# Attention outputs formed turned in half lanes, weighed by small spreading products

## The chip, the cores and the metric

The kernel runs on one core of a Trainium2 chip, as one program. TensorE (PE in the profile) multiplies, VectorE (DVE) and ScalarE (ACT) work element by element and empty PSUM, SyncE (SP) issues transfers. The metric is device time in microseconds of that core: the median of 3 runs.

## The reference

The program computes two blocks on 256 tokens of width 1024. The first is a block with a state space mixer, an attention with forget gates and a mixture of experts. The second has two layers, and each layer has three attention mixers, whose outputs go through projections and gates, and then a cross attention and a feed-forward part. The change is inside the three mixers of the second block, so it runs once in each of the two layers. What they compute for one block of 128 queries, cut to its core:

```python
def masked_probs(s, mask, sink=None):
    ...
    e = jnp.exp(s - m)
    denom = jnp.sum(e, axis=-1, keepdims=True)
    if sink is not None:
        denom = denom + jnp.exp(sink - m)
    return e / jnp.where(denom > 0, denom, 1.0)

# swa (8 heads of 64, 2 key heads), window 128
o = einsum('bgrqk,bkgd->bqgrd', masked_probs(s, mask, sink), vb)
# nsa: three branches, each weighed by a gate of its own
return g[..., 0:1] * o_cmp + g[..., 1:2] * o_sel + g[..., 2:3] * o_win
# mla: 8 heads
return einsum('bhqk,bkhd->bqhd', masked_probs(s, kpos <= t), v)
```

So each head's output is a product of unnormalised weights with the values, times one factor for each query and head: the reciprocal of the sum, and for the nsa branches the gate as well.

## The kernel before, in words

Each engine has a queue written out by hand (for TensorE from L659, ScalarE from L1829, VectorE from L2276); counting semaphores tie them. A PSUM bank is a `Bank` with two counters: `full`, raised by the engine that filled it, and `free`, raised by the one that emptied it; `claim(b, ...)` waits until the bank's last user is done. The bank of the outputs is O, that of the scores S (two banks), that of the turned weights PT (two banks), and X is a spare one.

The mixers of a layer are a pipeline of 18 steps, `MIXER_STEPS`: swa 0 to 3, sel 4 to 7, cmp 8 and 9, win 10 to 13, mla 14 to 17. A step is a kind, a group of four heads (`pp`) and a block of 128 queries (`qb`). Steps with `qb` 0 have one block of 128 keys, those with `qb` 1 two. The two cmp steps do all 8 heads on 16 compressed keys each.

TensorE does at step n, in this order: `mixer_turn(n)` transposes the weights of step n (L775, cmp L1314), the scores of step n+2 (L763), one or more `gate_part`s of 12 products of 128x512 each (L1282; these are a part of the gate projection and fill the time in which the others work), and `mixer_output(n)`: the outputs of step n (`output_step`, L785). There the turned weights of 128 keys x 128 queries are the stationary operand and 64 value columns move, so the output has queries in the lanes and head columns along a row. The cmp steps have one product of 128x512 (L1322). An fp32 product shows as two matmul records in the trace, a transpose as one.

VectorE does at step n: for a cmp step `total_blocks` (L3153 to L3160: sum, reciprocal, gate), `mixer_mask(n+2)` (L2366, L2369: scores with mask, and row maxima), `mixer_finish(n)` (`finish_step`: reciprocal L2390, gate L2394, and the multiply L2404 that empties O; cmp L3167, L3169), then the low parts of the gate weights (`make_gate_low`, L3074, one for each gate part of step n+2). Extra pieces stand at single steps: at step 0 the eight L3108, at step 15 `make_low("bra")`, a pass of 128x4096 over the weights of the first branch projection (L2314). ScalarE does the exponentials of step n+1 (L1900), empties PT (L2191) and the gate banks (L2170), and makes the high parts of the weights (L2145, L1876).

Behind the last step TensorE transposes the three finished outputs (L691, `turn_rows`), 8 blocks each in pairs of banks X and O, ScalarE rounds each to its high part (`turned_high`, L1887), VectorE takes the low part (`turned_low`, L2305), and TensorE starts the branch projections (L718, `product_wide`), "bra" first.

## Time and profile before

| | us |
|---|---|
| median of 3 runs | 1678.88 (1677.71 to 1680.25) |
| profiled execution | 1675.22 |
| its span | 1673.5 |
| TensorE busy | 1590.7 (95%) |
| VectorE busy | 939.6 (56%) |
| ScalarE busy | 654.3 (39%) |

The mean granted clock of TensorE is 0.988 of full speed. The first block ends near 577 us, the two layers of the second follow, near 577 to 1117 and 1117 to 1673. The mixer pipeline of the first layer lies at about 690 to 818 us, that of the second at 1228 to 1357. A row of the timeline has a start, a length, an engine, a line of the kernel, the operation and its tiles, and a count; a bracket at its end is idle time of the engine before it and what ended it. Successive matmuls overlap in the records, so their pitch (the distance of two starts) tells the rate, not their length.

### The profile page before, as it was taken

To read this page: it belongs to the slowest core of one execution; us is meant where nothing else is said; L and a number is where in the kernel's file an instruction comes from. 1 tells how busy PE (TensorE), PEld (TensorE's weight loads), DVE (VectorE), ACT (ScalarE), POOL (GpSimd) and SP (SyncE) were. 2 spreads that over 40 slices of the span, in tenths; PEclk is the share of its full clock that TensorE was granted. 3 is DMA by queue.
4 is the path that set the end of the run, shared out by engine and by line. 5 is a ranking of instruction groups with operands and counts; after the bars stand their busy time and mean duration, and the time that the engine had idled before them with its cause. 6 is when DMAs were issued, how large, how long until landed. Compare 5 with 4: busy or idle time off the path is not lost.

```text
span 1673.5 us, 22371 instructions
## 1 busy us (share of the span) xinstructions
PE 1590.7 (95%) x9359; PEld 1237.3 (74%) x9359; DVE 939.6 (56%) x1374; ACT 654.3 (39%) x960; POOL 27.1 (2%) x89
## 2 busy tenths in 40 slices
PE   5999999989999899999999999999999999999998
PEld 1998655454545377687888899978768878889986
DVE  3876676642222465556675566545466567556653
ACT  2543411111111243556545544335265744543441
POOL 1000010100000000000000000000000000000000
PEclk9999999999999999999999999999999999999999
DMA  9555519979999943333345355545424235435551
GB/s 309 189 186 201 202 52 332 386 289 414 411 423 381 353 142 129 102 137 109 133 152 180 123 192 172 191 154 192 154 76 152 101 130 191 157 130 185 202 181 71
DMA packets 153155, 333.33 MB, mean 199 GB/s; under 512 B 17764, under 2 KB 69222, under 8 KB 140774
## 3 DMA queue, kind: packets, MB, share of 16 engines
q1 hardware_dynamic: 147504, 326.94, 53.9%
q10 hardware_dynamic: 5558, 5.06, 0.9%
q8 instruction: 70, 1.15, 0.3%
q14 instruction: 23, 0.18, 0.0%
HBM read 330.94 MB, written 1.05 MB: 198 GB/s over the span
## 4 chain that ended last, share of the span: by engine, by line
PE 81%; DVE 9%; DMA 4%; ACT 4%; issue 1%; POOL 0%; ACTq 0%; POOLq 0%; DVEq 0%; SPq 0%
PE ps_g L737 19%; PE ps_g L718 15%; PE ps_g L1142 6%; PE ps_g L1282 6%; PE ps_s L1538 4%; PE ps_p L1538 3%; PE ps_o L785 3%; PE ps_g L878 3%; DVE ring_r L2314 2%; PE ps_p L718 2%; PE ps_o L1171 2%; DMA ring<-in_w_mod_dram 1%; PE ps_x L1171 1%; PE ps_p L775 1%; DMA arena<-in_w_up_dram 1%
## 5 line engine op out<-in xcount | busy, mean ns | idle before, releaser
L2314 DVE TENSOR_TENSOR ring_r<-ring,late_w 128x4096 fp32r<-128x4096 f32 (+1 forms) x50 | 216.9, 4339 | 153.3 <-ACT late_w L1876 153.3
L1876 ACT ACTIVATE late_w<-ring 128x4096 fp32r<-128x4096 f32 (+1 forms) x50 | 178.2, 3563 | 126.7 <-PE ps_p L1538 42.8
L737 PE MATMUL ps_g<-hf_high,ring_r 128*128 128x256 f32 x640 | 179.0, 280 | 0.0
L737 PE MATMUL ps_g<-hf_high,late_w 128*128 128x256 f32 x576 | 162.1, 281 | 0.0
L737 PE MATMUL ps_g<-h_t_r,late_w 128*128 128x256 f32 x576 | 161.3, 280 | 0.0
L737 PEld LDWEIGHTS ps_g<-hf_high,ring_r 128*128 128x128 f32 x640 | 122.0, 191 | 0.0
L737 PEld LDWEIGHTS ps_g<-h_t_r,late_w 128*128 128x128 f32 x576 | 108.6, 189 | 0.0
L737 PEld LDWEIGHTS ps_g<-hf_high,late_w 128*128 128x128 f32 x576 | 108.1, 188 | 0.0
L1900 ACT ACTIVATE arena<-arena,neg_max 128x256 f32<-128x256 f32 (+1 forms) x160 | 71.5, 450 | 40.9 <-DVE neg_max L2369 40.9
L1142 PE MATMUL ps_g<-arena 128*64 128x512 f32 x288 | 83.9, 592 | 0.0
L718 PE MATMUL ps_g<-early_w,first_low 128*128 128x512 f32 (+1 forms) x176 | 68.7, 390 | 3.8 <-ACT arena L1862 1.8
L785 PEld LDWEIGHTS ps_o<-arena 128*128 128x128 f32 x496 | 61.4, 192 | 13.2 <-issue 9.1
L1282 PE MATMUL ps_g<-gate_w,first_low 128*128 128x512 f32 x160 | 67.4, 421 | 1.6 <-ACT arena L2170 1.6
L718 PE MATMUL ps_g<-early_w,h_t_r 128*128 128x512 f32 (+1 forms) x176 | 68.6, 390 | 0.0
L2314 DVE TENSOR_TENSOR ring_r<-ring,early_w 128x4096 fp32r<-128x4096 f32 (+2 forms) x12 | 47.6, 3968 | 36.9 <-ACT early_w L1876 36.9
L718 PE MATMUL ps_g<-ring_r,first_low 128*128 128x512 f32 (+1 forms) x176 | 68.2, 387 | 0.0
L785 PE MATMUL ps_o<-arena 128*128 128x64 f32 (+1 forms) x496 | 61.5, 273 | 6.3 <-ACT arena L1915 3.1
L1282 PE MATMUL ps_g<-gate_w,h_t_r 128*128 128x512 f32 x160 | 63.1, 394 | 0.0
L1282 PE MATMUL ps_g<-ring_r,first_low 128*128 128x512 f32 x160 | 62.9, 393 | 0.0
L2314 DVE TENSOR_TENSOR ring_r<-ring,first_w 128x4096 fp32r<-128x4096 f32 x11 | 48.7, 4426 | 25.0 <-ACT first_w L1876 25.0
L3074 DVE TENSOR_TENSOR ring_r<-ring,gate_w 128x1024 fp32r<-128x1024 f32 x40 | 48.4, 1219 | 24.3 <-ACT gate_w L2145 23.9
L1142 PE MATMUL ps_g<-ring,arena 128*64 128x512 f32 x192 | 55.6, 593 | 2.3 <-issue 2.3
(697 smaller groups left out, 3707.1 us busy)
## 6 DMA issues: line engine op xcount, KB each, us to landing
...
```

Source lines behind the costliest of these rows:

```text
L718: ins = pe.matmul(b.ap[:, 0:n], x[:, k, tb * P:(tb + 1) * P], a[:, k, lo:lo + n], start=k == 0 and i == 0, stop=k == nk - 1 and i == len(b ...
L737: ins = pe.matmul(b.ap[:, (f % 2) * SEQ:(f % 2 + 1) * SEQ], a[:, k, f * P:(f + 1) * P], x[:, k, :], start=k == 0 and i == 0, stop=k == nk ...
L785: ins = pe.matmul(O.ap[:, i * width:(i + 1) * width], probs_t[:, i, b, :], v(step, i, b), start=b == 0, stop=b == kbs - 1)
L878: ins = pe.matmul(b.ap[:, :], x[:, k, tb * P:(tb + 1) * P], w[:, k, :], start=k == 0, stop=k == KD - 1)
L1142: ins = pe.matmul(b.ap[lanes, :], taken_t[:, k, lanes], w[k], start=k == 0, stop=k == KD - 1)
L1171: ins = pe.matmul(y.ap[lanes, :], hid_t[:, k, lanes], wd[:, k, half * HALF:(half + 1) * HALF], start=k == 0, stop=k == KF - 1)
L1282: ins = pe.matmul(G[tb].ap[:, :], x[:, 2 * q + k, tb * P:(tb + 1) * P], a[:, k, :], start=q == 0 and k == 0 and i == 0, stop=q == KD // 2 ...
L1538: ins = pe.matmul((S, PT)[tb].ap[:, half * HALF:(half + 1) * HALF], a[:, k, tb * P:(tb + 1) * P], x[:, k - 4 * c, half * HALF:(half + 1) * ...
L1876: act.activation(high_of(name, rnd)[:, 0:n], ring[:, slot, 0:n], ACT.Copy).then_inc(high_ready.sem, 1)
L1900: ins = act.activation(s, s, ACT.Exp, bias=neg_max[:, n % 2, i:i + 1], scale=-1.0, accum_out=den[:, n % 4, i:i + 1])
L2314: dve.tensor_tensor(ring_r[:, slot, 0:n], ring[:, slot, 0:n], high_of(name, rnd)[:, 0:n].bitcast(F32), ALU.subtract).then_inc(low_ready.se ...
L3074: dve.tensor_tensor(gate_piece(name, q, ring_r), gate_piece(name, q, ring), gate_high_w[q].bitcast(F32), ALU.subtract).then_inc(gate_low, 1)
```

## The change

The outputs are formed turned. In `turned_output` the 64 value columns of a head are the stationary operand and the turned weights of 128 queries move; the result has head columns in the lanes and queries along a row. Even heads of a group go to lanes 0 to 63 and odd ones to lanes 64 to 127, so two heads share the columns of one product. As a query's factor now differs along the row and not by lane, it has to be spread over lanes: four more products per step have the factor of a head, one number for each query, broadcast over 64 columns as stationary operand, and the identity moves. They write columns 256 to 511 of O. VectorE forms the factors ahead (`mixer_inverse`), and TensorE waits for them (`inverse_ready`) ahead of these four. `mixer_finish` then copies the spread factors to SBUF and multiplies (L3237, L3240 of the changed kernel; win adds a third operation) where it multiplied once.

The cmp steps scale the weights before they are turned (L3184), so the transposition of step 8 and 9 waits for `blocks_scaled`, and their output is four products of 128x128. The finished outputs lie turned in `heads_t`; the 24 transpositions of a layer behind the mixers go, ScalarE and VectorE take high and low part from SBUF, and the first branch projection waits for `heads_low_ready`. The banks' counts of uses change with that (`LAYER_USES`: O 45 to 42, X 30 to 27).

```diff
...
@@ -1309,9 +1312,27 @@
                     if step[0] != "cmp":
                         turn_probs("layer", step, l)
                         return
-                    pe.wait_ge(probs.sem, probs.at("layer", step_tag(step), l))
+                    pe.wait_ge(blocks_scaled, len(CMP_STEPS) * l + CMP_STEPS.index(step) + 1)
                     claim(PT, step_tag(step), l)
                     pe.transpose(PT.ap[:, 0:P], scores[:, n % 2, 0, 0:P], ident[:, :]).then_inc(PT.full, 1)
+
+                def turned_output(step, v):
+
+                    tag, kbs = step_tag(step), keys_of(step) // P
+                    claim(O, tag, l)
+                    pe.wait_ge(PT.free, PT.nth("layer", tag, l))
+                    for c in range(2):
+                        for b in range(kbs):
+                            for half in range(2):
+                                pe.matmul(O.ap[half * HD:(half + 1) * HD, c * P:(c + 1) * P], v(2 * c + half, b), probs_t[:, 2 * c + half, b, :],
+                                          start=b == 0, stop=b == kbs - 1)
+                    pe.wait_ge(inverse_ready, len(WEIGHED) * l + WEIGHED.index(step) + 1)
+                    inverse = rden[:, MIXER_STEPS.index(step) % 2, 0:4]
+                    for i in range(4):
+                        half, c = i % 2, 2 + i // 2
+                        ins = pe.matmul(O.ap[half * HD:(half + 1) * HD, c * P:(c + 1) * P], inverse[:, i:i + 1].broadcast_to([P, HD]), ident[:, :],
+                                        start=True, stop=True)
+                    ins.then_inc(O.full, 1)
 
...
@@ -1319,13 +1340,15 @@
                     if step[0] == "cmp":
                         claim(O, step_tag(step), l)
                         pe.wait_ge(PT.free, PT.nth("layer", step_tag(step), l))
-                        pe.matmul(O.ap[:, :], probs_t[:, 0, 0, :], cmp_v[:, :, :].rearrange("p h d -> p (h d)"), start=True, stop=True)\
-                            .then_inc(O.full, 1)
+                        v = cmp_v[:, :, :].rearrange("p h d -> p (h d)")
+                        for c in range(KF):
+                            ins = pe.matmul(O.ap[:, c * P:(c + 1) * P], v[:, c * P:(c + 1) * P], probs_t[:, 0, 0, :], start=True, stop=True)
+                        ins.then_inc(O.full, 1)
                     elif step[0] == "mla":
-                        output_step("layer", step, lambda s, i, b: mla_v[:, b, (4 * s[1] + i) * HD:(4 * s[1] + i + 1) * HD], l)
+                        turned_output(step, lambda i, b: mla_v[:, b, (4 * step[1] + i) * HD:(4 * step[1] + i + 1) * HD])
                     else:
                         at_v = {"swa": C_AV, "sel": C_VS, "win": C_VW}[step[0]]
-                        output_step("layer", step, lambda s, i, b: proj[:, b, at_v + HD * (i // 2):at_v + HD * (i // 2 + 1)], l)
+                        turned_output(step, lambda i, b: proj[:, b, at_v + HD * (i // 2):at_v + HD * (i // 2 + 1)])
...
@@ -1373,12 +1396,6 @@
                     mixer_output(n)
 
 
-                for name, src in (("a", o_a), ("b", o_b), ("c", o_c)):
-                    if name == "b":
-                        pe.wait_ge(rows.sem, rows.at("layer", "ob", l))
-                    else:
-                        pe.wait_ge(O.free, O.nth("layer", step_tag((SWA_STEPS if name == "a" else MLA_STEPS)[-1]), l))
-                    turn_rows(f"o{name}", [lambda tb, k=k, s=src: s[:, tb, k * P:(k + 1) * P] for k in range(KF)], l)
...
-                for name in "ab":
-                    turned("layer", f"o{name}", 2, l)
+                for i, name in enumerate("ab"):
+                    pe.wait_ge(heads_low_ready, 6 * l + 2 * i + 2)
                     product_wide("layer", f"br{name}", (o_high[name], o_low[name]), l)
...
-                turned("layer", "oc", 2, l)
+                pe.wait_ge(heads_low_ready, 6 * l + 6)
...
@@ -2209,7 +2226,12 @@
                 act.wait_ge(O.full, O.nth("layer", step_tag(MLA_STEPS[-1]), l))
                 act.dma_start(mem_rows[:, :, :], t["mem_2"][0].rearrange("(b p) n -> p b n", p=P)).then_inc(in_mem, 16)
                 for name in "abc":
-                    turned_high(f"o{name}", KF, o_high[name], l)
+                    if name == "b":
+                        act.wait_ge(rows.sem, rows.at("layer", "ob", l))
+                    else:
+                        act.wait_ge(O.free, O.nth("layer", step_tag((SWA_STEPS if name == "a" else MLA_STEPS)[-1]), l))
+                    for r in range(2):
+                        act.activation(o_high[name][:, 2 * r:2 * r + 2, :], heads_t[name][:, 2 * r:2 * r + 2, :], ACT.Copy).then_inc(x_high.sem, 1)
...
@@ -3159,15 +3181,37 @@
...
+                    dve.tensor_tensor(block_scores(n), block_scores(n), over(rden[:, n % 2, :], CMP), ALU.mult).then_inc(blocks_scaled, 1)
+
+                def block_of(step, chunks):
+                    return heads_t["b" if step[0] in ("sel", "cmp", "win") else "a" if step[0] == "swa" else "c"][:, chunks, step[2] * P:(step[2] + 1) * P]
 
                 def finish_blocks(n, step):
 
-                    tag, o = step_tag(step), o_b[:, step[2], :].rearrange("p (h d) -> p h d", d=HD)
+                    tag, o = step_tag(step), block_of(step, slice(0, KF))
+                    dve.wait_ge(O.free, O.nth("layer", step_tag(MIXER_STEPS[n - 1]), l))
                     dve.wait_ge(O.full, O.nth("layer", tag, l))
-                    dve.tensor_tensor(cmp_tmp, O.ap[:, :].rearrange("p (h d) -> p h d", d=HD), over(rden[:, n % 2, :], HD), ALU.mult).then_inc(O.free, 1)
+                    dve.tensor_tensor(o, o, O.ap[:, :].rearrange("p (c q) -> p c q", q=P), ALU.add).then_inc(O.free, 1)
                     dve.wait_ge(O.free, O.nth("layer", tag, l))
-                    st.done(dve.tensor_tensor(o, o, cmp_tmp, ALU.add))
-                    st.settle()
+
+                def mixer_inverse(n):
+
+                    step = MIXER_STEPS[n]
+                    if step[0] == "cmp":
+                        total_blocks(n, step)
+                        return
+                    total, inv = den[:, n % 4, 0:4], rden[:, n % 2, 0:4]
+                    dve.wait_ge(probs.sem, probs.at("layer", step_tag(step), l))
+                    if step[0] == "swa":
+                        st.done(dve.tensor_tensor(total, total, sink_e[:, n % 4, 4:8], ALU.add))
+                        st.settle()
+                    ins = dve.reciprocal(inv, total)
+                    if step[0] in ("sel", "win"):
+                        st.done(ins)
+                        st.settle()
+                        inv4 = inv.rearrange("p (f r) -> p f r", f=2)
+                        ins = dve.tensor_tensor(inv4, inv4, branch(1 + (step[0] == "win"), step), ALU.mult)
+                    ins.then_inc(inverse_ready, 1)
...
                 def mixer_finish(n):
 
                     step = MIXER_STEPS[n]
-                    if step[0] == "swa":
-                        finish_step("layer", step, crossed(o_a)(step), l)
-                    elif step[0] == "sel":
-                        finish_step("layer", step, crossed(o_b)(step), l, branch(1, step), first=True)
-                    elif step[0] == "cmp":
+                    if step[0] == "cmp":
                         finish_blocks(n, step)
-                    elif step[0] == "win":
-                        ins = finish_step("layer", step, crossed(o_b)(step), l, branch(2, step))
-                        if step == WIN_STEPS[-1]:
-                            ins.then_inc(rows.sem, 1)
-                        else:
-                            st.done(ins)
-                            st.settle()
+                        return
+                    pp = step[1]
+                    out_t = block_of(step, slice(2 * pp, 2 * pp + 2) if step[0] == "mla" else slice(pp, KF, 2))
+                    dve.wait_ge(O.full, O.nth("layer", step_tag(step), l))
+                    sums, weight = (O.ap[:, i * SEQ:(i + 1) * SEQ].rearrange("p (c q) -> p c q", q=P) for i in range(2))
+                    st.done(dve.tensor_copy(o_tmp[:, :, :], weight))
+                    st.settle()
+                    if step[0] != "win":
+                        dve.tensor_tensor(out_t, sums, o_tmp[:, :, :], ALU.mult).then_inc(O.free, 1)
+                        return
+                    dve.tensor_tensor(o_tmp[:, :, :], sums, o_tmp[:, :, :], ALU.mult).then_inc(O.free, 1)
+                    dve.wait_ge(O.free, O.nth("layer", step_tag(step), l))
+                    ins = dve.tensor_tensor(out_t, out_t, o_tmp[:, :, :], ALU.add)
+                    if step == WIN_STEPS[-1]:
+                        ins.then_inc(rows.sem, 1)
                     else:
-                        finish_step("layer", step, o_c[:, step[2], step[1] * SEQ:(step[1] + 1) * SEQ].rearrange("p (i d) -> p i d", d=HD), l)
+                        st.done(ins)
+                        st.settle()
...
                 for n, step in enumerate(MIXER_STEPS):
-                    if step[0] == "cmp":
-                        total_blocks(n, step)
+                    mixer_inverse(n)
                     if n + 2 < len(MIXER_STEPS):
                         mixer_mask(n + 2)
                     mixer_finish(n)
...
                 for name in "abc":
-                    turned_low(f"o{name}", KF, o_low[name], o_high[name], l)
+                    for r in range(2):
+                        dve.wait_ge(x_high.sem, x_high.at("layer", f"o{name}{r}", l))
+                        dve.tensor_tensor(o_low[name][:, 2 * r:2 * r + 2, :], heads_t[name][:, 2 * r:2 * r + 2, :],
+                                          o_high[name][:, 2 * r:2 * r + 2, :].bitcast(F32), ALU.subtract).then_inc(heads_low_ready, 1)
...
```

Lines of the changed kernel are shifted: L785 answers to L1327 and L1333, L1314 to L1317, L1322 to L1345, L763 to L766, L1282 to L1285, L3074 to L3096, L2404 to L3237 and L3240, L2314 to L2336.

TensorE at the end of step 7 and the start of step 8, before:

```order
L785 MATMUL ps_o<-arena 128x64 [waits p_free,o_free]
L785 MATMUL ps_o<-arena 128x64 x7
L1314 MATMUL ps_p<-ident,arena 128x128 [waits p_free,probs_ready]
L763 MATMUL ps_s<-arena 128x128 [waits s_free]
L763 MATMUL ps_s<-arena 128x128 x3
```

and after:

```order
L1327 MATMUL ps_o<-arena 64x128 [waits p_free,o_free]
L1327 MATMUL ps_o<-arena 64x128 x7
L1333 MATMUL ps_o<-ident,rden 64x128 [waits inverse_ready]
L1333 MATMUL ps_o<-ident,rden 64x128 x3
L1317 MATMUL ps_p<-ident,arena 128x128 [waits p_free,blocks_scaled]
L766 MATMUL ps_s<-arena 128x128 [waits s_free]
L766 MATMUL ps_s<-arena 128x128 x3
```

Eight products of step 7 have become twelve, and the transposition of step 8 now waits for VectorE's scaling instead of the exponentials.

VectorE at the same place, from `mixer_finish(7)` on, before:

```order
L2404 TENSOR_TENSOR arena<-ps_o,rden 128x2x128 [waits o_full,vector_steps]
L3074 TENSOR_TENSOR ring_r<-ring,gate_w_64 128x1024 [waits gate_high]
L3153 TENSOR_REDUCE den<-arena 128x8 [waits probs_ready]
L3155 TENSOR_SCALAR den<-den 128x8 [waits vector_steps]
L3157 RECIPROCAL rden<-den 128x8 [waits vector_steps]
L3160 TENSOR_TENSOR rden<-rden,branch_g 128x8 [waits vector_steps]
L2366 SCALAR_TENSOR_TENSOR arena<-ps_s,causal 128x4x128 [waits s_full,vector_steps]
L2369 TENSOR_REDUCE neg_max<-arena 128x4 [waits s_free]
L3167 TENSOR_TENSOR arena<-ps_o,rden 128x512 [waits o_full]
```

and after:

```order
L3237 COPY arena<-ps_o 128x256 [waits o_full]
L3240 TENSOR_TENSOR arena<-ps_o,arena 128x2x128 [waits vector_steps]
L3096 TENSOR_TENSOR ring_r<-ring,gate_w_64 128x1024 [waits gate_high]
L3175 TENSOR_REDUCE den<-arena 128x8 [waits probs_ready]
L3177 TENSOR_SCALAR den<-den 128x8 [waits vector_steps]
L3179 RECIPROCAL rden<-den 128x8 [waits vector_steps]
L3182 TENSOR_TENSOR rden<-rden,branch_g 128x8 [waits vector_steps]
L3184 TENSOR_TENSOR arena<-arena,rden 128x128 [waits vector_steps]
L2388 SCALAR_TENSOR_TENSOR arena<-ps_s,causal 128x4x128 [waits s_full]
L2391 TENSOR_REDUCE neg_max<-arena 128x4 [waits s_free]
L3194 TENSOR_TENSOR arena<-arena,ps_o 128x4x128 [waits o_full,o_free]
```

The scaling L3184 stands behind the finish of step 7 and a gate weight pass; before, the transposition of step 8 waited for nothing in this queue.

VectorE at steps 15 to 17 (`late_w_56` holds the weights of "bra"), after:

```order
L3237 COPY arena<-ps_o 128x256 [waits o_full]
L3240 TENSOR_TENSOR arena<-ps_o,arena 128x2x128 [waits vector_steps]
L3096 TENSOR_TENSOR ring_r<-ring,gate_w_66 128x1024 [waits gate_high]
L2336 TENSOR_TENSOR ring_r<-ring,late_w_56 128x4096 [waits high_ready]
L3208 RECIPROCAL rden<-den 128x4 [waits probs_ready]
L3237 COPY arena<-ps_o 128x256 [waits o_full]
L3240 TENSOR_TENSOR arena<-ps_o,arena 128x2x128 [waits vector_steps]
```

The reciprocal L3208 is that of step 16, behind the pass over the weights, as it was before; new is that TensorE's products of step 16 wait for it.

## Rows read from the trace of the kernel before

**Rows 1.** Windows, mixers: us, busy PE, PEld, DVE, ACT, POOL, clock, DMA, GB/s.

```profile
690.00:818.00 128.00, 121.57 (x814) 101.45 (x815) 81.99 (x143) 78.10 (x198) 0.00 (x0) 1.00 0.28 102
1228.00:1357.00 129.00, 122.97 (x814) 102.55 (x811) 82.13 (x144) 78.04 (x198) 0.00 (x0) 0.99 0.28 102
```

**Rows 2.** Chain, end of the first layer's mixers: start, us, what.

```profile
800.80 1.73 PE ps_o L785 x16
...
802.98 2.77 PE ps_g L1282 x12
805.75 0.84 PE ps_o L785 x8
```

**Rows 3.** Timeline, TensorE: full-width and half-width products; start, us, engine, line, tiles, xcount.

```profile
303.04 18.19 PE L878 MATMUL ps_g<-ring,arena 128*128 128x512 f32 x42
...
382.72 7.04 PE L1142 MATMUL ps_g<-arena 128*64 128x512 f32 x32
```

**Rows 4.** Timeline, TensorE, from half-wide to full-wide tiles.

```profile
709.76 0.51 PE L1282 MATMUL ps_g<-gate_w,first_low 128*128 128x512 f32 x1
710.10 0.39 PE L1282 MATMUL ps_g<-ring_r,first_low 128*128 128x512 f32 x1
```

**Rows 5.** Timeline, steps 7 and 8 of the mixers.

```profile
741.16 0.29 DVE L3148 TENSOR_TENSOR arena<-arena,neg_max 128x128 f32<-128x128 f32 x1
...
743.88 0.28 PE L1314 MATMUL ps_p<-ident,arena 128*128 128x128 f32 x1
...
744.15 0.42 DVE L2404 TENSOR_TENSOR arena<-ps_o,rden 128x256 f32<-128x256 f32 x1 [2.41 <-PE ps_o L785]
...
744.49 1.21 DVE L3074 TENSOR_TENSOR ring_r<-ring,gate_w 128x1024 fp32r<-128x1024 f32 x1
...
745.62 0.28 DVE L3153 TENSOR_REDUCE den<-arena 128x8 f32<-128x128 f32 x1
...
746.58 0.69 DVE L2366 SCALAR_TENSOR_TENSOR arena<-ps_s,causal 128x512 f32<-128x512 f32 x1
```

**Rows 6.** Timeline, steps 8 to 10.

```profile
751.25 0.27 PE L1314 MATMUL ps_p<-ident,arena 128*128 128x128 f32 x1
...
751.45 0.69 DVE L3167 TENSOR_TENSOR arena<-ps_o,rden 128x512 f32<-128x512 f32 x1 [3.46 <-PE ps_o L1322]
...
757.42 0.71 PE L763 MATMUL ps_s<-arena 64*128 64x128 f32 x8 [0.56 <-DVE arena L2366]
...
761.94 0.47 PE L1282 MATMUL ps_g<-gate_w,first_low 128*128 128x512 f32 x1 [0.81 <-ACT arena L2170]
```

**Rows 7.** Timeline, steps 15 to 17 and the first branch products.

```profile
804.12 4.42 DVE L2314 TENSOR_TENSOR ring_r<-ring,late_w 128x4096 fp32r<-128x4096 f32 x1
...
811.83 0.61 PE L691 MATMUL ps_x<-ident,arena 128*128 128x128 f32 x4
...
812.50 0.60 ACT L1887 ACTIVATE oa_high<-ps_x 128x512 fp32r<-128x512 f32 x1 [1.51 <-PE ps_x L691]
...
817.14 0.48 PE L718 MATMUL ps_g<-late_w,oa_high 128*128 128x512 f32 x1
...
821.57 4.43 DVE L2314 TENSOR_TENSOR ring_r<-ring,late_w 128x4096 fp32r<-128x4096 f32 x1 [2.83 <-ACT late_w L1876]
...
828.41 0.40 PE L718 MATMUL ps_g<-late_w,ob_high 128*128 128x512 f32 x1
```

**Rows 8.** Timeline, steps 0 and 1.

```profile
699.38 4.49 DVE L3108 TENSOR_TENSOR arena<-arena,g_col 64x256 f32<-64x256 f32 x8
...
705.26 0.71 PE L763 MATMUL ps_s<-arena 64*128 64x128 f32 x8 [0.39 <-DVE arena L2366]
```

**Rows 9.** Windows, second layer, TensorE at half clock.

```profile
1235.20:1238.60 3.40, 3.40 (x17) 2.90 (x18) 2.83 (x5) 2.88 (x12) 0.00 (x0) 0.50 0.00 0
```

**Rows 10.** Timeline, TensorE, first output of the first and the second layer.

```profile
696.72 1.08 PE L785 MATMUL ps_o<-arena 128*128 128x64 f32 x8 [1.52 <-ACT arena L2191]
...
1234.42 1.21 PE L785 MATMUL ps_o<-arena 128*128 128x64 f32 x8 [1.51 <-ACT arena L2191]
```

9 lines of the change are left out of this document (6 added, 3 removed).

## The prediction

> **What bounds the kernel now.** I first read the windows over the two mixer pipelines: TensorE is busy 121.6 of 128 us and 123.0 of 129, VectorE 82 and ScalarE 78 [rows 1]. So the pipelines move at TensorE's pace, and what TensorE gains or loses there shows, unless a wait for another engine takes it back. The two layers read alike, so I work out the first and double it. Second I read the chain of waits at the pipeline's end: it runs from one TensorE group to the next, 1.73 us for the output products of a step with two key blocks, 0.84 for one [rows 2]. Third, the timeline at the places where the order of instructions changes: steps 0 and 1, 7 to 9, and 15 to the first branch product. TensorE has little idle time there, and what it has is small (0.39, 0.56, 0.81 us) [rows 6, 8]. Everything below is on TensorE's own timeline; a plus is time lost.
>
> **The change part by part, one layer.**
>
> *A, the products.* Of the 16 weighed steps, 8 have two key blocks and 8 one. Before, 16 records in 1.73 us and 8 in 0.84, thus 0.107 each [rows 2]. After, two halves of the lanes are written in turn. Whether they run side by side is told by the nearest products of this kind: 32 of 128x512 into half the columns took 7.04 us, 0.22 each, where 42 of full width took 18.19, 0.43 each [rows 3]; a pair of halves costs what one full product does. So a pair with 128 columns moving takes 0.11. A step with two blocks has 8 products for the sums and 4 for the factors, two records each: 12 pairs, 1.32 us; with one block 8 pairs, 0.88. To this comes the change of tile width, twice per step. After half-wide products, the first full-wide one was followed at 0.34 us [rows 4], where the steady pitch is 2.77/12 = 0.23 [rows 2]: 0.11 for that alone, and as much again is possible ahead of the first. I take 0.31 per step for both changes, bounds 0 and 0.5. That gives 1.63 against 1.73 and 1.19 against 0.84: 8 x (-0.10) + 8 x 0.35 = +2.0. The cmp outputs become 8 records of about 0.11 for about as much time, +0.1 for both. A is +2.1; with no cost for the change of width -2.9, with 0.5 it is +5.1, and with halves that run one after the other (0.107 each, so 2.6 and 1.7 us and the same 0.31) +16.5.
>
> The Trainium skill (TensorEngine Tiling (Array Packing), Performance Considerations) advises exactly such a swap of the stationary and the moving operand where the moving side has 64 columns, for twice the rate. By it alone, with no factors and no change of width to pay, the products would take half of 1.73 and 0.84, some 10 us less per layer. The same page (Key Properties) says that changing the tiling mode drains the engine: a cost that each of these short groups pays twice. The trace agrees with both as far as it goes, by the 0.22 and the 0.34 above.
>
> *B, the wait of the cmp steps.* The transposition of step 8 now waits for the scaling on VectorE. Ahead of it VectorE has the finish of step 7, which can only begin when TensorE has ended step 7's products, one instruction before the transposition. Read from rows: VectorE saw the end of the products 0.27 us after TensorE went on (744.15 against 743.88); the multiply took 0.34 to the next start, the gate pass 1.13, the four small ones 0.96 [rows 5]. After the change: 0.27, a copy of the same size with the wait of the multiply for it (0.45), 0.34, 1.13, 0.96, and the scaling, for which the subtraction of the same 128x128 took 0.29 [rows 5]: 3.45 us in which TensorE stands. Queued behind the transposition are the scores of step 10 and the gate products, which could run. Step 9 likewise: 0.20 to VectorE's start (751.45 against 751.25), the finish 0.73, two gate passes 2.27, 0.96, 0.30: 4.45 [rows 5, 6]. Two waits of TensorE just behind, 0.56 for VectorE and 0.81 for ScalarE, whose reason is that those engines lag, go with it [rows 6]: -1.4. B is +6.5. From below it is bounded by 0, were VectorE ahead; from above by 7.9, without the part given back.
>
> *C, the factors of step 16.* Its reciprocal stands behind the weight pass of 4.42 us, begun at 804.12 [rows 7], now some 0.4 later. Before, nobody but VectorE cared. Now the four spreading products wait. TensorE's output of step 16 begins at 805.75 [rows 2] and gets through the sums at 806.3; the pass ends at 808.95 and the reciprocal near 809.2. C is +2.9, bounds 2 and 3.5.
>
> *D, steps 0 and 1.* Eight small operations hold VectorE from 699.38 for 4.49 us, and TensorE waits 0.39 for the mask behind them [rows 8]. The copy ahead of them (0.45) and the reciprocal with the addition of the sink, which now stand ahead of that mask (0.4), come on top: +0.85. At step 12 the transpositions for mla claim the bank O, which a finish longer by the copy's 0.45 frees: +0.3. In the other steps the finish and the factors have the 2.8 to 5.5 us of gate products as cover; VectorE has 46 idle us, and the longer finish costs it some 16 x 0.45 = 7.
>
> *E, the end.* The 24 transpositions, in TensorE's way with waits for the banks, lasted from 811.83 to 817.14: 5.3 us. In their place TensorE waits behind its last product for the first high part, which ScalarE began 0.67 later (812.50) and did in 0.60, and then two low parts of 0.69 on VectorE, as long as its pass over 128x512 [rows 6, 7]: near 2.7 with the handovers. VectorE's copy and multiply of step 17 (0.27 + 0.8) lie beside ScalarE's part. E is -2.6. Late next would be the weights of the second branch: their low pass began 4.4 us after the first branch product (821.57 against 817.14), took 4.43, and was wanted at 828.41, 2.4 us later than it ended [rows 7]. ScalarE now has all six high parts after that point, which takes about 0.8 of the 2.4. So the gain stays.
>
> Sum: 2.1 + 6.5 + 2.9 + 1.15 - 2.6 = +10.05 us per layer.
>
> *F, the clock.* The three new stalls are 3.5, 4.5 and 2.9 us, longer than any in the pipeline now. In the second layer TensorE idled 1.51 us before its first output; from 1235.2 the granted clock was 0.50, that is 1.2 GHz, for 3.4 us. In the first layer 1.52 us idle at the same place had no such effect [rows 1, 9, 10]. One fall costs half of 3.4, 1.7 us. With idle times two to three times as long I count a fall after two of the three stalls: +3.4 per layer, bounds 0 and 5.1. (The Trainium skill, TensorE: Matmul & The Clock Gate, likewise has the clock fall to half after idling, and so speaks against an edit that trades work for waits.)
>
> Two layers: 2 x (10.05 + 3.4) = +26.9 us. The profiled execution, 1675.2, would become 1702.1. The median of the timed runs lies 3.7 above the profiled one; on that basis 1678.9 + 26.9 = 1705.8, and I say 1706.
>
> **The rivals.**
>
> *The clock holds.* For it: the first layer's 1.52 us. Then 2 x 10.05, 1699.0.
>
> *The halves don't run side by side* for such short products. The rows for it are of 512 columns; at 128 the weight load, not the moving side, sets the pitch, and the trace has no half-wide product of 128 columns. Then A is 16.5 in place of 2.1: 2 x (24.45 + 3.4) = +55.7, 1734.6.
>
> *VectorE is ahead and none of its new waits bites: not slower.* The place is the queue of VectorE between O's filling and the scaling of step 8 and 9, and the pass ahead of step 16. If its work is finished whenever TensorE asks, B, C and D fall away: 2.1 - 2.6 = -0.5 per layer, 1677.9, no change; if the change of width were free besides, 2 x -5.5, 1667.9. It decides from the point where the scaling ends 3.4 us earlier than I have it. For it speaks only VectorE's 46 idle us; against it the queue's order, in which the scaling stands behind a finish that needs the product just ended.
>
> *The stalls are given back*, partly. TensorE waits at step 8, but VectorE and ScalarE catch up, and later waits in the pipeline shrink. I counted 1.4; if 3 us more per layer come back and the clock falls once, 2 x (7.05 + 1.7) = +17.5, 1696.4.
>
> **How the numbers follow.** The forecast 0.48, the clock holds 0.2, stalls given back 0.16, halves in series 0.09, VectorE ahead 0.07. The range must hold the first three with their bounds: low 1691 (given back and no fall: 1678.9 + 2 x 7.05 = 1693, less 2 for A), high 1721 (A at +5.1 and three falls: 2 x (13.05 + 5.1) = +36.3 gives 1715, and 6 for what the queue's delay costs elsewhere). A measurement tells this kernel from no change at about 0.2%, 3.4 us. Faster by more: 0.03, the part of the last rival with free changes of width. Within: 0.04, its other part. Slower: 0.93.
>
> **What would show it.** At step 8 and 9 TensorE idle for 3.5 and 4.5 us before L1317, ended by VectorE; at step 16 idle for near 3 us between the sums L1327 and the spreading products L1333; the records of a two-block step in 1.6 us; the first branch product 2.7 us after the last output; granted clock 0.50 in some stretches behind the stalls. I would be wrong if a group of 16 half-wide records took 1.7 us by itself (halves in series), or if the idle time before L1317 were under 1 us.

## The result

The changed kernel takes 1708.89 us (median of 6 runs, 1706.79 to 1711.23), the kernel before 1678.61 us in the same series: 1.018 of it, interval 1.0165 to 1.0194. That is 30.3 us slower. The forecast was 1706, and 26.9 us slower.

The page of the changed kernel, part 1: TensorE has 15.7 us more of busy time, the span is 36.0 us longer.

```profile
PE 1606.4 (94%) x9591; PEld 1234.9 (72%) x9591; DVE 950.3 (56%) x1406; ACT 653.8 (38%) x960; POOL 27.1 (2%) x89
```

The profiled execution of before lay at the short end of its runs (1675.2), and this one took 1711.2. To tell the layers from that, I match VectorE's passes over the split weights (L2314 before, L2336 after), of which both kernels have the same number in the same order. The timeline of VectorE, first before, then after: the last such pass ahead of the first layer's mixers, one behind them, the last one ahead of the second layer's, and one behind those.

```profile
636.39 4.13 DVE L2314 TENSOR_TENSOR ring_r<-ring,early_w 128x3808 fp32r<-128x3808 f32 x1 [7.08 <-ACT early_w L1876]
...
857.15 4.42 DVE L2314 TENSOR_TENSOR ring_r<-ring,late_w 128x4096 fp32r<-128x4096 f32 x1
...
1172.19 4.13 DVE L2314 TENSOR_TENSOR ring_r<-ring,early_w 128x3808 fp32r<-128x3808 f32 x1 [5.65 <-ACT early_w L1876]
...
1384.83 4.42 DVE L2314 TENSOR_TENSOR ring_r<-ring,late_w 128x4096 fp32r<-128x4096 f32 x1
```

```profile
639.78 4.13 DVE L2336 TENSOR_TENSOR ring_r<-ring,early_w 128x3808 fp32r<-128x3808 f32 x1 [7.08 <-ACT early_w L1893]
...
875.96 4.42 DVE L2336 TENSOR_TENSOR ring_r<-ring,late_w 128x4096 fp32r<-128x4096 f32 x1
...
1190.81 4.13 DVE L2336 TENSOR_TENSOR ring_r<-ring,early_w 128x3808 fp32r<-128x3808 f32 x1 [5.63 <-ACT early_w L1893]
...
1420.90 4.41 DVE L2336 TENSOR_TENSOR ring_r<-ring,late_w 128x4096 fp32r<-128x4096 f32 x1
```

The distances are 3.4, 18.8, 18.6 and 36.1 us. So 3.4 us arose in code that the change doesn't touch, 15.2 us from the first of these passes to the third, the first layer's stretch, and 17.4 from the third to the fourth, the second's. These two numbers, taken between far passes, are what I use below for a layer. Together they are 32.7 us, more than the 30.3 of the medians: the profiled execution of before is 3.4 us under its median, that of the changed kernel 2.3 us above.

The windows of the changed kernel: the first layer's mixers as a whole, and then four short stretches in them (us, busy of PE, PEld, DVE, ACT, POOL, granted clock, DMA share, GB/s).

```profile
690.00:835.00 145.00, 127.94 (x949) 100.50 (x949) 88.46 (x165) 79.71 (x200) 0.00 (x0) 0.95 0.24 83
748.30:751.80 3.50, 0.30 (x6) 0.05 (x2) 2.98 (x8) 0.70 (x2) 0.00 (x0) 1.00 0.94 329
752.80:756.20 3.40, 3.40 (x11) 2.66 (x10) 1.38 (x2) 0.67 (x1) 0.00 (x0) 0.54 1.06 393
765.40:769.80 4.40, 4.33 (x14) 2.90 (x15) 1.78 (x3) 1.22 (x2) 0.00 (x0) 0.50 0.00 0
825.20:828.20 3.00, 3.00 (x13) 2.76 (x12) 0.93 (x3) 0.99 (x1) 0.00 (x0) 0.51 0.01 3
```

TensorE was busy 121.6 of 128 us before [rows 1]; now it is idle for 17 of 145. The second row is one of the new waits: TensorE stands, VectorE works through 2.98 of 3.5 us. The last three rows lie directly behind such waits, and there the granted clock is 0.50 to 0.54 of full speed, 1.2 GHz.

The timeline at the end of step 7 and in steps 8 and 9, to be read beside [rows 5] and [rows 6]:

```profile
748.64 0.42 DVE L3237 COPY arena<-ps_o 128x256 f32<-128x256 f32 x1 [1.85 <-PE ps_o L1333]
...
751.53 0.29 DVE L3184 TENSOR_TENSOR arena<-arena,rden 128x128 f32<-128x128 f32 x1
...
751.88 0.33 PE L1317 MATMUL ps_p<-ident,arena 128*128 128x128 f32 x1 [3.29 <-DVE arena L3184]
...
761.17 0.69 DVE L3194 TENSOR_TENSOR arena<-arena,ps_o 128x512 f32<-128x512 f32 x1 [6.86 <-PE ps_o L1345]
...
765.13 0.29 DVE L3184 TENSOR_TENSOR arena<-arena,rden 128x128 f32<-128x128 f32 x1
...
765.47 0.48 PE L1317 MATMUL ps_p<-ident,arena 128*128 128x128 f32 x1 [4.41 <-DVE arena L3184]
```

The transposition of step 8 comes 3.29 us after TensorE went idle, that of step 9 4.41 us, both released by the scaling L3184. In between VectorE is never idle: finish, gate passes, sums, scaling.

Steps 15 to the first branch product, which answer to [rows 7]:

```profile
819.86 4.42 DVE L2336 TENSOR_TENSOR ring_r<-ring,late_w 128x4096 fp32r<-128x4096 f32 x1
...
824.19 0.17 DVE L3208 RECIPROCAL rden<-den 128x4 f32<-128x4 f32 x1
...
824.41 0.86 PE L1333 MATMUL ps_o<-ident,rden 128*64 128x128 f32 x8 [2.60 <-DVE rden L3208]
...
825.20 1.97 PE L778 MATMUL ps_p<-ident,arena 128*128 128x128 f32 x8
...
831.32 0.61 PE L1333 MATMUL ps_o<-ident,rden 128*64 128x128 f32 x8
...
832.43 1.15 ACT L2234 ACTIVATE oa_high<-arena 128x512 fp32r<-128x512 f32 x2 [1.24 <-PE ps_o L1333]
...
834.44 0.50 PE L721 MATMUL ps_g<-late_w,oa_high 128*128 128x512 f32 x1 [2.52 <-DVE oa_low L3276]
```

The spreading products of step 16 wait 2.60 us for the reciprocal behind the weight pass; the eight transpositions behind them take 1.97 us, at half clock, where the same number at full clock takes 1.09 (the third row of the next fence). The first branch product starts 3.1 us after the last group of products began.

Two ordinary steps, one with one key block and one with two, on TensorE:

```profile
716.80 0.66 PE L1327 MATMUL ps_o<-arena 128*64 128x128 f32 x8
717.29 0.61 PE L1333 MATMUL ps_o<-ident,rden 128*64 128x128 f32 x8
717.83 1.09 PE L778 MATMUL ps_p<-ident,arena 128*128 128x128 f32 x8
722.89 1.09 PE L1327 MATMUL ps_o<-arena 128*64 128x128 f32 x16
723.82 0.61 PE L1333 MATMUL ps_o<-ident,rden 128*64 128x128 f32 x8
724.35 0.66 PE L778 MATMUL ps_p<-ident,arena 128*128 128x128 f32 x4
```

The short step's products take 1.03 us from the first start to the next group's (717.83 - 716.80), where they took 0.84; the long step's 1.46, where they took 1.73 [rows 2]. Sixteen half-wide records take 0.93 us (723.82 - 722.89), half of what as many full-width ones took. That fits halves that run side by side; products that are short by themselves would look the same, and the run with the halves in series tells the two apart.

### The profile page after: what moved, and what is told of

It is laid out like the page before. It is cut to its first block, busy times and chain, and to the rows that moved or that the text cites. A ratio compares the mean times of both kernels' runs of the same rounds, so it can differ in the third digit from the quotient of the medians.

```text
span 1709.5 us, 22823 instructions
## 1 busy us (share of the span) xinstructions
PE 1606.4 (94%) x9591; PEld 1234.9 (72%) x9591; DVE 950.3 (56%) x1406; ACT 653.8 (38%) x960; POOL 27.1 (2%) x89
## 3 DMA queue, kind: packets, MB, share of 16 engines
q8 instruction: 72, 1.18, 0.3%
## 4 chain that ended last, share of the span: by engine, by line
PE 81%; DVE 10%; DMA 4%; ACT 4%; issue 1%; ACTq 0%; POOL 0%; POOLq 0%; DVEq 0%; SPq 0%
PE ps_g L740 19%; PE ps_g L721 16%; PE ps_g L1145 6%; PE ps_g L1285 6%; PE ps_s L1555 4%; PE ps_p L1555 3%; PE ps_g L881 3%; PE ps_p L721 2%; DVE ring_r L2336 2%; PE ps_o L1174 1%; PE ps_s L721 1%; PE ps_x L1174 1%; DMA ring<-in_w_mod_dram 1%; PE ps_p L778 1%; DMA arena<-in_w_up_dram 1%
## 5 line engine op out<-in xcount | busy, mean ns | idle before, releaser
L2336 DVE TENSOR_TENSOR ring_r<-ring,late_w 128x4096 fp32r<-128x4096 f32 (+1 forms) x50 | 216.9, 4338 | 152.4 <-ACT late_w L1893 152.4
L1285 PE MATMUL ps_g<-gate_w,first_low 128*128 128x512 f32 x160 | 70.6, 441 | 0.0
L2336 DVE TENSOR_TENSOR ring_r<-ring,early_w 128x4096 fp32r<-128x4096 f32 (+2 forms) x12 | 47.6, 3968 | 36.8 <-ACT early_w L1893 36.8
L1285 PE MATMUL ps_g<-ring_r,first_low 128*128 128x512 f32 x160 | 65.8, 411 | 0.0
L1285 PE MATMUL ps_g<-gate_w,h_t_r 128*128 128x512 f32 x160 | 65.3, 408 | 0.0
L2336 DVE TENSOR_TENSOR ring_r<-ring,first_w 128x4096 fp32r<-128x4096 f32 x11 | 48.7, 4425 | 25.3 <-ACT first_w L1893 25.0
L3096 DVE TENSOR_TENSOR ring_r<-ring,gate_w 128x1024 fp32r<-128x1024 f32 x40 | 48.4, 1218 | 24.3 <-ACT gate_w L2162 23.9
L740 PE MATMUL ps_g<-first_high,first_w 128*128 128x256 f32 x192 | 54.9, 286 | 0.0
L740 PE MATMUL ps_g<-first_low,first_w 128*128 128x256 f32 x192 | 54.8, 286 | 0.0
## 6 DMA issues: line engine op xcount, KB each, us to landing
ring<-in_w_mod_dram SPq DMA_DIRECT2D x10, 2048.0 KB, 11.7
arena<-in_w_gate_dram SPq DMA_DIRECT2D x16, 1024.0 KB, 13.5
```

Source lines behind the costliest of these rows:

```text
L740: ins = pe.matmul(b.ap[:, (f % 2) * SEQ:(f % 2 + 1) * SEQ], a[:, k, f * P:(f + 1) * P], x[:, k, :], start=k == 0 and i == 0, stop=k == nk ...
L1285: ins = pe.matmul(G[tb].ap[:, :], x[:, 2 * q + k, tb * P:(tb + 1) * P], a[:, k, :], start=q == 0 and k == 0 and i == 0, stop=q == KD // 2 ...
L2336: dve.tensor_tensor(ring_r[:, slot, 0:n], ring[:, slot, 0:n], high_of(name, rnd)[:, 0:n].bitcast(F32), ALU.subtract).then_inc(low_ready.se ...
L3096: dve.tensor_tensor(gate_piece(name, q, ring_r), gate_piece(name, q, ring), gate_high_w[q].bitcast(F32), ALU.subtract).then_inc(gate_low, 1)
```

## The experiments

The second column is the median; "layers" is the time of each layer's stretch against before, measured by the matched passes of the two profiles. All ratios are to the kernel before, run on the same chip in the same series; its median was 1678.6 to 1680.5 in them. A profile shows one execution, which lies up to 4.4 us from the median of its runs, so the medians say what a version is worth and the layers show where it arises.

| run | us | ratio (interval) | layers 1, 2 |
|---|---|---|---|
| changed kernel | 1708.9 | 1.018 (1.0165 to 1.0194) | +15.2, +17.4 |
| waits filled | 1695.4 | 1.010 (1.0076 to 1.0118) | +8.5, +9.1 |
| cmp factors early | 1684.4 | 1.0026 (1.0014 to 1.0038) | +3.5, +4.2 |
| step 16 factors early | 1699.4 | 1.012 (1.0102 to 1.0133) | +8.7, +9.4 |
| all factors early | 1673.6 | 0.9965 (0.9947 to 0.9983) | -2.6, -3.6 |
| before, cmp weights scaled | 1700.2 | 1.013 (1.0106 to 1.0153) | +10.8, +10.9 |
| halves in series | 1681.4 | 1.0007 (0.9997 to 1.0018) | +2.6, +0.1 |
| weights scaled | 1701.9 | 1.013 (1.0106 to 1.0151) | +11.5, +11.6 |
| scaled, first heads early | 1691.8 | 1.007 (1.0054 to 1.0082) | +9.2, +8.3 |
| scaled in place | 1691.1 | 1.0065 (1.0045 to 1.0084) | +5.3, +6.1 |
| all factors and heads early | 1670.4 | 0.994 (0.9923 to 0.996) | -5.2, -4.4 |
| short steps scaled | 1686.7 | 1.004 (1.003 to 1.0058) | +4.0, +6.3 |
| five steps scaled | 1663.3 | 0.991 (0.9894 to 0.9923) | -7.5, -8.4 |

**The waits filled.** Is the half clock a cost of its own?

```diff
+                def filler(count, last):
+
+                    pe.wait_ge(X.free, X.nth("layer", last, l))
+                    for _ in range(count):
+                        pe.matmul(X.ap[:, 0:P], ident[:, :], ident[:, :], start=True, stop=True)
...
+                    filler(18 if n % 2 else 13, "cmpkv")
                     pe.wait_ge(blocks_scaled, len(CMP_STEPS) * l + CMP_STEPS.index(step) + 1)
...
+                    if step == MIXER_STEPS[16]:
+                        filler(10, "mk2")
                     pe.wait_ge(inverse_ready, len(WEIGHED) * l + WEIGHED.index(step) + 1)
...
+                filler(9, "mk2")
                 for i, name in enumerate("ab"):
                     pe.wait_ge(heads_low_ready, 6 * l + 2 * i + 2)
```

> The changed kernel with products of the identity by itself into the idle bank X while TensorE waits: 13 ahead of the transposition of step 8, 18 ahead of that of step 9, 10 ahead of the spreading products of step 16, 9 ahead of the first branch product. What they write is read by nobody; each set is a little shorter than the wait it stands in. Theory (the waits cost their own length and then, each, some 1.7 us of half clock behind them): the waits end when they did, the clock stays at 1.00, 8 x 1.7 = 13.6 us less, about 1695. Rival (half the clock isn't what the idle time brings, or the slower stretch behind a wait has another cause, as a change of tile width or busy transfers): no change, 1709, or a little more.

Measured: 1695.4, 13.5 us less than the changed kernel. TensorE's timeline around step 8, and the window over the same mixers:

```profile
747.40 0.61 PE L1342 MATMUL ps_o<-ident,rden 128*64 128x128 f32 x8
747.94 3.17 PE L1324 MATMUL ps_x<-ident 128*128 128x128 f32 x26
751.30 0.33 PE L1318 MATMUL ps_p<-ident,arena 128*128 128x128 f32 x1 [0.19 <-DVE arena L3194]
```

```profile
690.00:830.00 140.00, 134.68 (x1048) 108.14 (x1047) 88.73 (x163) 80.45 (x202) 0.00 (x0) 1.00 0.25 88
```

The transposition of step 8 comes 3.9 us after the spreading products, as in the changed kernel (751.88 against 747.99), so the wait is no shorter; but the clock is 1.00 throughout. The first layer is 6.8 us shorter by the matched passes, the second 8.4. This is the price of the half clock, and it is real: 13.5 of 30.3 us by the medians, nearly half of what the change cost.

**The cmp factors early.** VectorE treats steps 8 and 9 ahead of the finish of the step before.

```diff
-                    mixer_inverse(n)
+                    if n == 0:
+                        mixer_inverse(0)
+                    elif not (MIXER_STEPS[n][0] == "cmp"):
+                        mixer_inverse(n)
                     if n + 2 < len(MIXER_STEPS):
                         mixer_mask(n + 2)
+                    if n + 1 < len(MIXER_STEPS) and (MIXER_STEPS[n + 1][0] == "cmp"):
+                        mixer_inverse(n + 1)
                     mixer_finish(n)
```

> The changed kernel, but VectorE sums and scales the weights of steps 8 and 9 ahead of the finish of the step before, not behind it; nothing else moves. Theory (the queue ahead of the scaling is the cost of the cmp wait): both waits go, 3.35 + 4.57 us, less 1.6 us of old waits that come back, and the half clock behind them, 1.6 + 2.2: 10.1 us per layer, about 1689. Rival (the time went into the longer and width-changing products, the wait only gathers what would be waited for elsewhere): under 6 us less in all, 1703 or more.

Measured: 1684.4, 24.5 us less, 11.7 and 13.2 per layer. The wait of the two transpositions is gone from the list of waits. It is more than expected because the old waits of [rows 6] (0.56 and 0.81 us) did not come back: the sums of a cmp step no longer stand ahead of the next mask. In the second layer more half clock went with the waits as well.

**The factors of step 16 early**, by the same edit with `n == 16` and `n + 1 == 16` in the two conditions.

> The changed kernel, but the factors of step 16 are formed ahead of the finish of step 15, and so ahead of the weight pass of 4.4 us; nothing else moves. Theory: the wait of 2.8 us at step 16 goes and the half clock behind it (1.7): 4.5 us per layer, 1708.9 - 9 = 1700. Rival (the wait comes back at the next point, the weights of the first branch or the exponentials): 1705 or more.

Measured: 1699.4, 9.5 us less, 4.7 per layer, where 4.5 was expected. The profiled execution took 1695.3, the shortest of the four, and shows 6.5 and 8.1 us less. In the first layer the rest is at the next wait. TensorE's timeline at the first branch product, and the window behind it:

```profile
824.94 0.61 PE L1333 MATMUL ps_o<-ident,rden 128*64 128x128 f32 x8
...
828.06 0.50 PE L721 MATMUL ps_g<-late_w,oa_high 128*128 128x512 f32 x1 [2.52 <-DVE oa_low L3281]
...
828.39 0.39 PE L721 MATMUL ps_g<-ring_r,oa_high 128*128 128x512 f32 x1
```

```profile
828.10:832.20 4.10, 4.10 (x18) 3.34 (x19) 2.31 (x4) 4.10 (x4) 0.00 (x0) 1.00 1.02 418
```

The wait for the first heads' low part is as long as in the changed kernel (2.52 us), but the clock stays at 1.00 behind it. In the changed kernel it fell there too:

```profile
834.40:838.50 4.10, 4.06 (x11) 3.20 (x12) 2.40 (x4) 4.10 (x4) 0.00 (x0) 0.58 1.02 420
```

That does not mean that the wait ahead decides it. In the second layer of this same profile the same wait (2.50 us, up to 1374.58), again with none ahead of it, did bring the half clock:

```profile
1374.60:1379.20 4.60, 4.60 (x13) 3.65 (x14) 2.33 (x4) 4.60 (x4) 0.00 (x0) 0.63 1.02 420
```

What the second layer gained besides is a half clock ahead of the mixers that the changed kernel had there and this execution did not. The price of such a wait varies, and not by its length alone.

**All factors early.** The factors of step n+1 are formed ahead of the finish of step n, for every n.

```diff
-                    mixer_inverse(n)
+                    if n == 0:
+                        mixer_inverse(0)
                     if n + 2 < len(MIXER_STEPS):
                         mixer_mask(n + 2)
+                    if n + 1 < len(MIXER_STEPS):
+                        mixer_inverse(n + 1)
                     mixer_finish(n)
```

> The changed kernel with the factors of every step formed one finish earlier (those of step n+1 ahead of the finish of step n), so those of step 16 stand ahead of the weight pass and those of step 1 ahead of the eight small operations. Theory: beside what the early cmp factors give, the 2.8 us of step 16 with 1.7 of half clock and 0.6 at step 1 go, 5 us per layer more: about 1679, no more than 2 us from the kernel before, since the dearer short steps (+1.6), the shorter end (-2.7) and one half clock behind the end (+1.5) nearly cancel. Rival (waiting for the exponentials earlier holds VectorE up): no better than the early cmp factors alone, 1689 or more.

Measured: 1673.6, 35.3 us less than the changed kernel and below the kernel before, 0.9965 of it. The same instructions, in another order of one queue, turn 1.8% slower into 0.35% faster. That is 5 us less than expected. I had let 1.6 us of old waits per layer come back and one half clock follow the wait at the end. The old waits are not in this trace; and the wait at the end stayed (2.52 and 2.50 us), but the granted clock is 1.00 over both layers' mixers, which the second layer of the run above shows to be partly luck. Dearer products (+1.6), the shorter end (-2.7) and the old waits (-1.4) make -2.5 per layer; the first layer shows -2.6.

**One part alone on the kernel before.** The cmp weights are scaled before they are turned, nothing else.

```diff
-                    pe.wait_ge(probs.sem, probs.at("layer", step_tag(step), l))
+                    pe.wait_ge(blocks_scaled, len(CMP_STEPS) * l + CMP_STEPS.index(step) + 1)
...
+                    dve.tensor_tensor(block_scores(n), block_scores(n), over(rden[:, n % 2, :], CMP), ALU.mult).then_inc(blocks_scaled, 1)
...
+                    dve.wait_ge(O.free, O.nth("layer", step_tag(MIXER_STEPS[n - 1]), l))
                     dve.wait_ge(O.full, O.nth("layer", tag, l))
-                    dve.tensor_tensor(cmp_tmp, ..., over(rden[:, n % 2, :], HD), ALU.mult).then_inc(O.free, 1)
+                    dve.tensor_tensor(o, o, O.ap[:, :].rearrange("p (h d) -> p h d", d=HD), ALU.add).then_inc(O.free, 1)
                     dve.wait_ge(O.free, O.nth("layer", tag, l))
-                    st.done(dve.tensor_tensor(o, o, cmp_tmp, ALU.add))
-                    st.settle()
```

> The kernel before with one part of the change alone: the cmp weights are scaled on VectorE before they are turned, and TensorE's transpositions of steps 8 and 9 wait for that; the finish of a cmp step is one addition. Theory: waits of 0.27 + 0.34 + 1.13 + 0.96 + 0.30 = 3.0 us and 0.2 + 0.7 + 2.3 + 0.96 + 0.3 = 4.5, less 1.6 of old waits, and 3.8 of half clock: 9.7 per layer, about 1698. Rival (the part is worth what its instructions take): within 2 us of the kernel before.

Measured: 1700.2, 10.8 and 10.9 us per layer, with one VectorE instruction of 0.29 us more and one of 0.69 less per cmp step. The list of waits on TensorE names it:

```profile
PE ps_p L1315 <- DVE arena L3163: 14.6, 4, 4.4
```

That is 7.3 us per layer of idle time, less the old waits; the rest is half clock. In each layer one fall of the clock has nothing to do with this wait: behind 1.51 us of idle time at the first output in the first layer, behind 2.04 us ahead of the mixers in the second. By the starts of TensorE's gate products around the cmp steps, 9.9 of the first layer's 10.8 us arise there. The medians give 20.9 of the change's 30.3 us, the first layer 9.9 of 15.2: about two thirds of the cost is the cmp steps' wait with its half clock.

**The halves in series.** In the version with all factors early, all products into lanes 0 to 63 come before those into lanes 64 to 127.

```diff
-                    for c in range(2):
-                        for b in range(kbs):
-                            for half in range(2):
+                    for half in range(2):
+                        for c in range(2):
+                            for b in range(kbs):
...
-                    for i in range(4):
+                    for i in (0, 2, 1, 3):
```

> The version with all factors early (1673.6), with the same half-wide products in another order: of a step, first all that write lanes 0 to 63, then all that write lanes 64 to 127, where the two alternated. If alternating halves run side by side (0.055 us per record in the profile) and a half by itself runs at the 0.11 of a full-wide product, 24 records take 2.6 in place of 1.3 us and 16 take 1.75 in place of 0.9: 8 x 1.3 + 8 x 0.85 = 17 us per layer, about 1708. If a half-wide product is short by itself, whatever stands next to it, the time stays at 1674.

Measured: 1681.4, 7.9 us more than with the halves alternating, a quarter of the 34 us expected. TensorE's timeline of one long step:

```profile
721.96 1.25 PE L1327 MATMUL ps_o<-arena 128*64 128x128 f32 x13
722.95 0.32 PE L1333 MATMUL ps_o<-ident,rden 128*64 128x128 f32 x1
723.05 0.27 PE L1327 MATMUL ps_o<-arena 128*64 128x128 f32 x1
723.11 0.27 PE L1333 MATMUL ps_o<-ident,rden 128*64 128x128 f32 x1
723.91 0.65 PE L778 MATMUL ps_p<-ident,arena 128*128 128x128 f32 x4
```

Records of one half start 0.109 us apart, by the single records of the trace. But those of the other half, written down behind them, begin beside them: from 722.95 on those of L1333 (the spreading products of the first half) and of L1327 (the second half's sums, which stand ahead of them) alternate at 0.055 us. The whole takes 1.95 us in place of 1.46. In a short step the order costs 0.05. My 17 us per layer took the halves to be in strict order, and the trace shows that TensorE takes products from further behind when they go to the other half. Both expected outcomes were wrong; that halves of one step run side by side stands.

**The weights scaled in every step.** No spreading products, no copy: VectorE multiplies the weights by their factors before they are turned.

```diff
+                    pe.wait_ge(blocks_scaled, len(MIXER_STEPS) * l + n + 1)
                     if step[0] != "cmp":
                         turn_probs("layer", step, l)
...
+                    nk = keys_of(step)
+                    s4 = scores_of(step, n)[:, 0:4, 0:nk]
+                    dve.tensor_tensor(s4, s4, over(inv, nk), ALU.mult).then_inc(blocks_scaled, 1)
...
                     mixer_finish(n)
+                    if n + 2 < len(MIXER_STEPS):
+                        mixer_scale(n + 2)
```

> The changed kernel with every step treated as the cmp steps are, but early: VectorE multiplies the weights by their factors before they are turned (for step n+2, behind the finish of step n), so the four spreading products and the copy go, and the finish is one copy or one addition. Theory (the spreading products cost TensorE 0.44 us in each of 16 steps, and VectorE has room): 7 us per layer less than with the factors early, 1673.6 - 14 = about 1660. Rival (VectorE's added passes, 8 of 1.2 and 8 of 0.7 us per layer less the copies, with waits for the exponentials in its queue, set the pace): 1673 or more.

Measured: 1701.9, so the rival. The waits, VectorE's own and the two kinds that TensorE has for VectorE:

```profile
DVE rden L3202 <- ACT arena L1911: 32.6, 20, 2.3
...
PE ps_s L766 <- DVE arena L2382: 10.3, 7, 2.7
...
PE ps_p L778 <- DVE arena L3210: 6.0, 6, 2.4
```

VectorE stands for the exponentials of step n+2 20 times, and the next mask and finish are queued behind it. With the first heads early as well:

> As the version with scaled weights, and besides the high and low part of the first mixer's output are made in steps 16 and 17 (its place in SBUF is exchanged with that of the second), so the first branch product need not wait for the last output. Theory: the 2.6 us behind the last product of the mixers go, in each layer: 5 us less than the version with scaled weights, more where that wait brought half the clock. Rival (what is late next, the low weights of the branch or the banks, keeps TensorE waiting as long): no change.

Measured: 1691.8, 10 us less by the medians, twice the 5 expected without a gain in clock. The two profiles show 2.3 and 3.3 us per layer, but the one of this version is the slowest of its six runs (1696.2); which share is the clock is not separated. With the scaling moved to where the early factors stand (`mixer_inverse(n + 1)` scales too):

> All weights scaled before they are turned, as in the run with scaled weights, but the pass for step n+1 stands where the version with early factors forms them (behind the mask of n+2, ahead of the finish of n), and the first heads' parts are made in steps 16 and 17. If what slowed the run with scaled weights was that its queue stood waiting for exponentials of step n+2 with the finish of the step and the next mask behind it, TensorE's waits go and the spreading products with them: 1673.6 - 14 - 5 = about 1655. If it was VectorE's sheer work (5.6 us in a step with two key blocks against TensorE's 5.3), it stays above 1673.

Measured: 1691.1. TensorE now waits 24.2 us, 11 times, all at the transposition:

```profile
PE ps_p L779 <- DVE arena L3226: 24.2, 11, 3.9
```

Neither place works for all steps. VectorE's sheer work is not the limit on average, 98 of 140 us busy over the first layer's mixers; what TensorE waits for is where the scaling stands in that queue at single steps (2.39, 3.95, 1.63 and 3.40 us in the first layer).

**The first heads early.** High and low part of the first mixer's output are made in steps 16 and 17, in the version with all factors early; the high part changes its place in SBUF with that of the second mixer.

```diff
+                    if n == len(MIXER_STEPS) - 2:
+                        for r in range(2):
+                            act.activation(o_high["a"][:, 2 * r:2 * r + 2, :], heads_t["a"][:, 2 * r:2 * r + 2, :], ACT.Copy).then_inc(x_high.sem, 1)
...
-                for name in "abc":
+                for name in "bc":
```

> The version with all factors early (1673.6), and the high and low part of the first mixer's output made in steps 16 and 17. The wait of 2.6 us behind the last product goes in each layer: about 1668; if another wait (low weights, banks, half clock at a place that was spared) takes its place, 1673.

Measured: 1670.4, where 1668 was expected. By the matched passes 2.6 us less in the first layer and 0.8 in the second, in which the clock fell once ahead of the mixers (1192.7) and had not in the version without this edit. The two intervals overlap, so the sign is known from the profile more than from the times.

**Where scaling pays.** From the version with the first heads early: the weights are scaled, where the early factors are formed, in the 8 short steps only, and then in 5 of them. The line for the 5:

```diff
-        WEIGHED = [step for step in MIXER_STEPS if step[0] != "cmp"]
+        SCALED = [step for step in MIXER_STEPS if step[0] == "cmp" or MIXER_STEPS.index(step) in (4, 6, 12, 14, 16)]
+        WEIGHED = [step for step in MIXER_STEPS if step not in SCALED]
```

> As the version with the first heads early, and in the 8 steps of one key block per layer VectorE scales the weights (0.7 us more, less the copy of 0.45) in place of the spreading products; the long steps keep these. Theory: 8 x 0.44 us of TensorE per layer go at 8 x 0.25 of VectorE, 7 us less than the version with the first heads early: about 1661. If a wait for scaled weights takes their place: 1668 or more.

Measured: 1686.7. The timeline of step 2 shows why:

```profile
703.74 4.53 DVE L3138 TENSOR_TENSOR arena<-arena,g_col 64x256 f32<-64x256 f32 x8
...
708.31 1.23 DVE L2396 SCALAR_TENSOR_TENSOR arena<-ps_s,windowed 128x1024 f32<-128x1024 f32 x1
...
711.50 0.69 DVE L3226 TENSOR_TENSOR arena<-arena,rden 128x512 f32<-128x512 f32 x1
...
712.25 1.11 PE L779 MATMUL ps_p<-ident,arena 128*128 128x128 f32 x4 [3.52 <-DVE arena L3226]
```

VectorE's eight small operations, a mask of two passes, then the scaling: TensorE waits 3.52 us where the spreading products would have taken 0.44.

> As the version with the first heads early, and the weights scaled on VectorE in place of the spreading products in 5 of the short steps, 4, 6, 12, 14 and 16: not in 0, 2 and 10, where VectorE's queue made TensorE wait for the scaled weights (3.5 us at step 2, 1.9 at step 10). Theory (the spreading products cost TensorE 0.44 us each time, and VectorE's pass costs nothing where it isn't late): 10 x 0.44 = 4.4 us less than the version with the first heads early, 1670.4 - 4.4 = 1666. Rival (the pass is late in these steps too): 1670 or more.

Measured: 1663.3, 0.991 of before (0.9894 to 0.9923), the fastest of all. Against the first heads early the layers are 2.3 and 3.9 us shorter; five times 0.44 is 2.2. The second layer's excess is about the one half clock ahead of its mixers (1.7 us) that the version with the first heads early had and this one lacks, so by the profiles about 4.5 us of the 7 between the two medians are the edit's, as expected.

## Why the prediction was right

The steps, with what the first layer shows (seen at TensorE's starts):

| step | forecast per layer | measured |
|---|---|---|
| A, products and change of width | +2.1 | +1.6 |
| B, cmp waits, less old waits | +6.5 | +6.3 |
| C, factors of step 16 | +2.9 | +2.8 |
| D, steps 1 and 12 | +1.15 | +0.8 |
| E, the end | -2.6 | -2.7 |
| F, half clock | +3.4 | +6.8 |

*A.* The two ordinary steps above give 1.46 and 1.03 us; the gate product ahead of them is followed 0.09 later than before, and the transpositions behind them start 0.05 more apart. So 1.60 for a long step and 1.17 for a short one, against 1.73 and 0.84: 8 x (-0.13 + 0.33) = +1.6. Twelve and eight pairs at 0.11 are 1.32 and 0.88, so the changes of width cost 0.28 per step, close to the 0.31 that I took.

*B.* 3.29 and 4.41 us of idle time (3.35 and 4.57 by starts), where 3.45 and 4.45 were forecast, each by the same chain of rows. Of the old waits TensorE got back 1.6, counted with their start gaps, in place of 1.4. 

*C, D, E.* 2.60 idle at step 16; at step 1 0.85 idle for the reciprocal behind the eight small operations, and 0.2 from the later start, of which 0.4 comes back at the scores behind it; 0.2 at step 12; the first branch product at 3.1 after the start of the spreading products, 2.5 of it idle.

*F* is the term that was mis-sized. I let the clock fall after two of three waits. It fell after all three, and after the wait at the end as well, which I had not counted as one: it is shorter than what it replaces [rows 7], but it has no transpositions in it. Filling the waits put the price at 6.8 and 8.4 us per layer, twice my 3.4 and more, and over the 5.1 that I gave as its bound for three falls. So the steps of the first layer add up to 15.6 where I had 13.45, and they would add up to more, had A and D not come out 0.9 us cheaper than forecast.

That the forecast of the median misses by only 3 us is in part luck. The two profiled executions are 32.7 us apart in the layers alone, 6 above my 26.9, and the medians 30.3.

The measured column adds up to 15.6, the passes say 15.2. In the second layer two things differ that the change doesn't touch: the clock fell behind 1.99 us of idle time ahead of the mixers, where 1.81 us had not brought it before (1.7 us), and did not fall at the first output, where it had [rows 9, 10] (1.5 us less). Most of the rest of the 2.2 us between the layers is longer half clock, behind step 8 above all (2.8 us lost against 1.6).

The rivals: that the clock holds is false. That VectorE is ahead is false as the kernel stands and true with the queue reordered. That the halves don't run side by side is false; its price was also added up wrongly: 24 and 16 records in 2.6 and 1.7 us, with 0.31 each, are 8 x (1.18 + 1.17) = 18.8 us more per layer and not 16.5, which would have made the rival some 1739. That the stalls are given back is false beyond the 1.6.
